# Last normalisation of five token tiles: product and offset split between ScalarE, VectorE and an adding DMA

## The reference, cut to what matters

```
x = layer_norm(ALPHA * x + mixer(x), ln1_g, ln1_b)
x = layer_norm(ALPHA * x + moe(x), ln2_g, ln2_b)

layer_norm(x, g, b) = (x - mean(x)) * rsqrt(var(x) + eps) * g + b
```

## Time and profile before

| | |
|---|---|
| median of three runs | 1285.62 us |
| profiled execution, its own time | 1287.54 us |
| its span, first to last instruction | 1285.7 us |
| TensorE busy | 1217.3 us, 95% |
| VectorE busy | 732.6 us, 57% |
| ScalarE busy | 579.2 us, 45% |
| GpSimd busy | 197.2 us, 15% |
| mean granted TensorE clock | 0.974 of full |
| the SP queue's transfers | 47.1% of the 16 DMA engines' span |
| GpSimd's transfers | 10.2% |

### The profile page before, as it was taken

One profiled execution on the slowest core, in us unless ns is written; L12 is line 12 of the kernel. 1 busy time (PEld: TensorE's weight loads), 2 busy tenths in 40 slices (PEclk: granted clock), 3 DMA queues, 4 the chain that ended last, 5 costly groups with the idle time before them and its releaser, 6 DMA issues.

```text
span 1285.7 us, 22049 instructions
## 1 busy us (share of the span) xinstructions
PE 1217.3 (95%) x8045; PEld 1090.7 (85%) x8045; DVE 732.6 (57%) x1790; ACT 579.2 (45%) x1416; POOL 197.2 (15%) x244
## 2 busy tenths in 40 slices
PE   6999999999999999998898999998799999999992
PEld 6998798888888888886677888897799999999892
DVE  3111455655665556556666887447566656656377
ACT  3221344544454444445543443220366766667464
POOL 0000001200210021011101122000213333333222
PEclk9999999999999999999798999899799999999996
DMA  5444664374536344565264333442799999999773
GB/s 185 160 127 129 168 144 100 82 185 94 130 88 174 95 108 104 138 146 169 70 199 165 132 142 115 159 153 66 248 304 277 282 288 280 270 280 292 195 291 131
DMA packets 157986, 220.69 MB, mean 172 GB/s; under 512 B 40608, under 2 KB 110496, under 8 KB 157856
## 3 DMA queue, kind: packets, MB, share of 16 engines
q1 hardware_dynamic: 147168, 180.80, 47.1%
q0 software_dynamic: 8192, 29.36, 10.2%
q10 hardware_dynamic: 2544, 9.44, 1.9%
HBM read 139.05 MB, written 50.63 MB: 148 GB/s over the span
## 4 chain that ended last, share of the span: by engine, by line
PE 82%; DVE 6%; issue 3%; ACT 3%; DMA 3%; DVEq 1%; SPq 1%; POOL 1%; ACTq 0%; POOLq 0%
PE bank L843 19%; PE bank L845 18%; PE bank L844 18%; PE bank L944 9%; PE bank L837 5%; PE bank L931 5%; PE bank L922 4%; PE bank L923 3%; PE bank L1064 2%; ACT b_work L1317 1%; DMA acc_scratch<-d_work,dstc 1%; DVE w_o L1677 1%; ACT w_o L1332 1%; DVE d_work L2086 1%; DVE d_work L2084 1%
## 5 line engine op out<-in xcount | busy, mean ns | idle before, releaser
L1317 ACT ACTIVATE b_work<-b_work 128x256 f32<-128x256 f32 (+3 forms) x288 | 148.0, 514 | 246.3 <-DVE b_work L1658 246.2
L843 PE MATMUL bank<-xgT_hi,w_gu_hi 128*128 128x224 f32 (+1 forms) x704 | 197.8, 281 | 4.4 <-ACT d_work L1550 2.3
L844 PE MATMUL bank<-xgT_lo,w_gu_hi 128*128 128x224 f32 (+1 forms) x704 | 196.5, 279 | 0.0
L845 PE MATMUL bank<-xgT_hi,w_gu_lo 128*128 128x224 f32 (+1 forms) x704 | 196.4, 279 | 0.0
L1667 DVE COPY b_work<-bank 128x256 f32<-128x256 f32 (+2 forms) x256 | 112.7, 440 | 116.8 <-PE bank L931 116.2
L843 PEld LDWEIGHTS bank<-xgT_hi,w_gu_hi 128*128 128x128 f32 x704 | 136.9, 195 | 6.6 <-issue 3.1
L2177 POOL CAST Q<-Q 128x512 fp32r<-128x512 f32 x48 | 52.2, 1118 | 576.0 <-DVE w_k_lo L1624 342.5
L844 PEld LDWEIGHTS bank<-xgT_lo,w_gu_hi 128*128 128x128 f32 x704 | 136.9, 194 | 0.7
L845 PEld LDWEIGHTS bank<-xgT_hi,w_gu_lo 128*128 128x128 f32 x704 | 136.9, 194 | 0.0
L931 PE MATMUL bank<-keep,b_work 128*128 128x128 f32 x608 | 115.8, 276 | 13.1 <-ACT b_work L1317 13.1
L931 PEld LDWEIGHTS bank<-keep,b_work 128*128 128x128 f32 x608 | 79.7, 140 | 51.0 <-ACT b_work L1317 22.5
(11 more groups left out here) (210 smaller groups left out, 2833.5 us busy)
## 6 DMA issues: line engine op xcount, KB each, us to landing
d_work<-in_w_gate SPq DMA_DIRECT2D x32, 512.0 KB, 8.7
d_work<-in_w_up SPq DMA_DIRECT2D x32, 512.0 KB, 9.6
d_work<-in_w_down SPq DMA_DIRECT2D x16, 1024.0 KB, 9.7
Q<-stage_hi SPq DMA_DIRECT2D x96, 128.0 KB, 2.4
Q<-stage_lo SPq DMA_DIRECT2D x96, 128.0 KB, 2.4
o_scratch<-b_work SPq DMA_DIRECT2D x36, 264.0 KB, 3.2
c_work<-o_scratch SPq DMA_DIRECT2D x12, 792.0 KB, 5.1
raw_w<-in_w_in SPq DMA_DIRECT2D x26, 256.0 KB, 4.2
```

What stands on the lines that cost most here:

```text
L843: nc.tensor.matmul(o, w_hi, x_hi, start=first, stop=False)
L844: nc.tensor.matmul(o, w_hi, x_lo, start=False, stop=False)
L845: return nc.tensor.matmul(o, w_lo, x_hi, start=False, stop=last)
L1317: nc.scalar.activation(prob[:, u % 2, 0:n], prob[:, u % 2, 0:n], ACT.Exp, scale=-1.0, bias=o[:, HD:HD + 1], accum_out=o[:, HD + 1:HD + 2])\
```

## The change

It has four parts. (1) Five tiles, 7, 5, 8, 9 and 10 (`Z_SUM`), are finished in another way: ScalarE's new `z_norm` makes (x - mean) * rstd2 in one pass over the tile, behind a tiny instruction for -mean * rstd2; VectorE's `z_out` makes only the product with g (one `tensor_tensor` where there were two instructions); and the offset b is added by the output itself. (2) For that, SP writes b into the output rows of the five tiles early, with five DMAs of 512 KB from the row `ln2_b` in DRAM, repeated 128 times, which stand in SP's list directly ahead of the zeros (L625). GpSimd later adds each finished tile to these rows with a DMA that accumulates (`add_out`): tile 7 behind the norm factor of tile 10, the other four behind that of tile 11. (3) The sum of tiles 6 to 11 is no longer a pass of ScalarE: `add_shared` puts out the sum of each half of the row, and two tiny ScalarE instructions with accumulators make the means. (4) The orders change: on VectorE `z_out(7)` stands between `add_shared` of tile 10 and that of tile 11; on ScalarE each `z_norm` stands behind the `z_stats` of the next tile.

```diff
+        Z_SUM = (7, 5, 8, 9, 10)
+        zparts = tri[:, 104:116].rearrange("p (t c) -> p t c", c=2)
+        shift = tri[:, 116:128]
@@ SP, ahead of the zeros and of pair(0)
+            for t in Z_SUM:
+                sp.dma_start(out_t[t], ln2_b.partition_broadcast(P)).then_inc(S["offsets_st"], 16)
+
             sp.wait_ge(S["zeros_ready"], 1)
@@ SP, end
             for n, t in enumerate(Z_ORDER):
-                sp.wait_ge(S["fin_ready"], n + 1)
-                sp.dma_start(out_t[t], base[:, t, :]).then_inc(S["out_st0"], 16)
-            sp.wait_ge(S["out_st0"], 16 * TILES)
+                if t not in Z_SUM:
+                    sp.wait_ge(S["fin_ready"], n + 1)
+                    sp.dma_start(out_t[t], base[:, t, :]).then_inc(S["out_st0"], 16)
+            sp.wait_ge(S["offsets_st"], 16 * len(Z_SUM))
+            sp.wait_ge(S["out_st0"], 16 * (TILES - len(Z_SUM)))
+            sp.wait_ge(S["sums_st"], 16 * len(Z_SUM))
@@ ScalarE, z_stats
-                nc.scalar.activation(zjunk, base[:, t, :], ACT.Copy, accum_out=zsum[:, c])
-                act.drain()
-                nc.scalar.activation(minus_mean[:, c], zsum[:, c], ACT.Copy, scale=-1.0 / D)
-                nc.scalar.activation(mean_32[:, c], zsum[:, c], ACT.Copy, scale=-1.0 / D / 32)
+                if t < 2 * EARLY:
...
+                else:
+                    nc.scalar.activation(zjunk[:, 0:2], zparts[:, t - 2 * EARLY, :], ACT.Copy, scale=-1.0 / D,
+                                         accum_out=minus_mean[:, c])
+                    nc.scalar.activation(zjunk[:, 2:4], zparts[:, t - 2 * EARLY, :], ACT.Copy, scale=-1.0 / D / 32,
+                                         accum_out=mean_32[:, c])
                 act.drain()
+            def z_norm(t):
+
+                c = slice(t, t + 1)
+                act.wait_ge(S["z_rstd"], Z_ORDER.index(t) + 1)
+                nc.scalar.activation(shift[:, c], minus_mean[:, c], ACT.Copy, scale=rstd2[:, c])
+                act.drain()
+                nc.scalar.activation(base[:, t, :], base[:, t, :], ACT.Identity, scale=rstd2[:, c], bias=shift[:, c])\
+                  .then_inc(S["z_norm"], 1)
@@ ScalarE, end
-            for t in (5, 8, 9, 10, 11):
-                z_stats(t)
+            z_stats(5)
+            z_norm(7)
+            z_stats(8)
+            z_norm(5)
+            z_stats(9)
+            z_norm(8)
+            z_stats(10)
+            z_norm(9)
+            z_stats(11)
+            z_norm(10)
@@ VectorE
-                    last = V.scalar_tensor_tensor(b, bank[4 + 2 * half + c][:], 1.0 / ALPHA, b, ALU.mult, ALU.add)
+                    sums = {"accum_out": zparts[:, 2 * (tile - EARLY) + half, c:c + 1]} if tile >= EARLY else {}
+                    last = V.scalar_tensor_tensor(b, bank[4 + 2 * half + c][:], 1.0 / ALPHA, b, ALU.mult, ALU.add, **sums)
@@ VectorE, z_out
+                if t in Z_SUM:
+                    dve.wait_ge(S["z_norm"], Z_SUM.index(t) + 1)
+                    V.tensor_tensor(base[:, t, :], base[:, t, :], ln2g, ALU.mult).then_inc(S["fin_ready"], 1)
+                    return
@@ VectorE, end
-            for half in range(2):
-                add_shared(end, EARLY + LATE - 1, half)
-            for t in (7, 5, 8, 9, 10, 11):
+            add_shared(end, EARLY + LATE - 1, 0)
+            z_out(7)
+            add_shared(end, EARLY + LATE - 1, 1)
+            for t in (5, 8, 9, 10, 11):
                 z_out(t)
@@ GpSimd
+            def add_out(t):
+
+                if t == Z_SUM[0]:
+                    pool.wait_ge(S["offsets_st"], 16 * len(Z_SUM))
+                pool.wait_ge(S["fin_ready"], Z_ORDER.index(t) + 1)
+                pool.dma_start(out_rows[t], base[:, t, :], accum_op=ALU.add).then_inc(S["sums_st"], 16)
+
@@ GpSimd, in the loop over Z_ORDER, behind the norm factor, and behind the loop
+                if t == Z_SUM[-1]:
+                    add_out(Z_SUM[0])
+            for t in Z_SUM[1:]:
+                add_out(t)
```

More of the change, by code:

```diff
@@ L360, in encoder_layer @@
             cum_need cum_made cum_read ej_ready id_need idm_made table_ready ids_col dst_col gathers_begun stores_begun g_ld late_ld
-            gcol_ready ln2_loaded z_var z_bn z_eps z_rstd fin_ready out_st0""".split()
+            gcol_ready ln2_loaded z_var z_bn z_norm offsets_st sums_st z_eps z_rstd fin_ready out_st0""".split()
         names += [f"acc_ld{t}" for t in range(TILES)]
@@ L1570, in z_stats @@
                 act.drain()
-                nc.scalar.activation(zjunk, base[:, t, :], ACT.Copy, accum_out=zsum[:, c])
-                act.drain()
-                nc.scalar.activation(minus_mean[:, c], zsum[:, c], ACT.Copy, scale=-1.0 / D)
-                nc.scalar.activation(mean_32[:, c], zsum[:, c], ACT.Copy, scale=-1.0 / D / 32)
+                if t < 2 * EARLY:
+                    nc.scalar.activation(zjunk, base[:, t, :], ACT.Copy, accum_out=zsum[:, c])
+                    act.drain()
+                    nc.scalar.activation(minus_mean[:, c], zsum[:, c], ACT.Copy, scale=-1.0 / D)
+                    nc.scalar.activation(mean_32[:, c], zsum[:, c], ACT.Copy, scale=-1.0 / D / 32)
+                else:
[3 more added lines that the diff above has]
+                                         accum_out=mean_32[:, c])
                 act.drain()
@@ L2256, in _ @@
             add_to_tokens(end)
+            out_rows = out.rearrange("(t p) d -> t p d", p=P)
+            def add_out(t):
[3 more added lines that the diff above has]
+                pool.dma_start(out_rows[t], base[:, t, :], accum_op=ALU.add).then_inc(S["sums_st"], 16)
             for n, t in enumerate(Z_ORDER):
```

## The result

The changed kernel is slower: 1302.86 us, median of five runs (1300.66 to 1305.16), against 1283.66 for the kernel before in five runs (1281.78 to 1286.1). The ratio is 1.0146 [1.0131, 1.0161], so 19 us. The prediction said 1292.1 and 1282 to 1298: the direction was right, the size lay outside the range.

What follows compares the result with a forecast made beforehand. VectorE was taken to bound the last stage, with the chain through TensorE before it. Beginning loses 10.4 us, end gains 3.9: +6.5 on the median 1285.62 gives 1292.1 us, range 1282 to 1298 for 8 in 10.

Steps and rivals of the forecast that it cites:

- The bound at the end: Last norms: VectorE bounds this stage; five fewer instructions remove 6.8 us, its chain ends at 1274.9, that branch gains 7.7.
- The sums: Ahead of the last shared product: shorter `z_stats` on ScalarE let the last Silu start earlier, of which 1.35 us arrive.
- The stall at the beginning: Attention start, 150 us: offsets ahead of `dup` into `KB` delay its landing and idle TensorE; 10.4 us lost (6.4 to 13.8).
- the clock term: After the stall near 160 us, TensorE restarts at 1.2 in place of 2.4 GHz: about 2.0 us lost (0 to 4).
- I take the slower middle, 8.4 us: Offsets in SP's queue near 150 us: 2.62 MB at 311 GB/s delay what follows by 8.4 us (6.4 to 9.8).
- The adding DMAs: End, GpSimd branch: four adding DMAs behind the last norm factor at 1271.5 end at 1281.8; gain 3.9 us (-1 to 7).
- I take 1.6 and 5.0, between the loaded rows and the plain store since the queues are empty here: End: each adding DMA costs GpSimd 1.6 us to issue and takes 5.0 us to landing.
- The "0.5" behind the landing: End: the span was to end 0.5 us behind the last adding DMA's landing, the last part of the sum 1281.8.
- The third rival: End: adding DMAs replace VectorE as bound, at 1.91 us each and 11.1 to landing; span end 1288.8, time 1299.1; chance 0.10.
- Behind it I see no stall that would take the delay up again: After the attention's beginning: the chain stays on TensorE for hundreds of us, so the beginning's delay is not regained.

Runs made afterwards that it cites:

- 14.0 alone: Kernel before plus only the five offset DMAs from the repeated `ln2_b` row, ahead of the zeros: 1300.72 us, ratio 1.0128.
- With distinct rows: Kernel before plus five DMAs ahead of the zeros, each copying 128 different rows of x instead of one repeated row: 1295.47 us, ratio 1.0088.
- three early additions with spread offsets: Changed kernel with offsets spread over attention passes, only tiles 7, 5, 8 finished the new way, adding DMAs issued earlier: 1277.52 us, ratio 0.9943.
- two early: Changed kernel with offsets spread over attention passes, only tiles 7 and 5 finished the new way, adding DMAs issued earlier: 1280.02 us, ratio 0.9968.
- Without the addition: Changed kernel with offsets spread over attention passes, GpSimd's five final DMAs writing tiles without adding: 1279.48 us, ratio 0.9965.

## Why the prediction was right or wrong

**The bound at the end: right.** VectorE's chain was the bound, and it shortened as said: its end was put at 1274.9 and came at 1274.1 in the time of the kernel before. So did ScalarE: the last `z_norm` was to end at 1270.7 and ended at 1282.74 - 12.62 = 1270.1. The cost of a `z_stats` and `z_norm` together was put at 3.5 us and measured 3.37 (1281.50 less 1278.13).

**The sums: right.** 1.35 us were to arrive of a shorter ScalarE list, and the wait fell by 1.35 us, 1.94 to 0.59. That TensorE's end came 3.0 us earlier owes 1.6 us to a lower clock that only the profile of the kernel before has.

**The stall at the beginning: mechanism right, rate wrong.** Queue, waiting engines and idle TensorE came as described, and the clock term was 1.8 us where 2.0 was said. The step that failed is "I take the slower middle, 8.4 us". It gave the offsets the rate of the stretch, 311 GB/s, with 9.8 as the upper bound from a copy between distinct rows. They took 12.5 us here and 14.0 alone, which is 2.62 MB at 210 and 187 GB/s. The nearest row for a repeated row had 374 GB/s, but that was a load into SBUF. With distinct rows the forecast held to 0.2 us. So the beginning lost 14.3 where 10.4 was said and 13.8 was the worst: 3.9 us.

**The adding DMAs: the price was put in the wrong place.** The prediction costed GpSimd's issue at 1.6 us each and gave every one 5.0 us to landing. The term was 1271.5 + 3 x 1.6 + 5.0 + 0.5 = 1281.8. In the time of the kernel before (less 12.62) the last issue began at 1271.7, 4.6 us earlier than the 1276.3 of the sum. From there to landing it took 13.3 us, 8.3 more than said, and behind the landing came 3.1 us and not 0.5, 2.6 more. In all 8.3 + 2.6 - 4.6 = 6.3 us, which turns a gain of 3.9 into a loss of 2.4. The step that failed is "I take 1.6 and 5.0, between the loaded rows and the plain store since the queues are empty here": the landing was taken as a latency that each DMA has for itself. It is throughput: each adding DMA of 512 KB holds all 16 DMA engines for about 3.0 us, so those issued 0.88 us apart queue behind each other. The "0.5" behind the landing failed too: it is what a store of SP's leaves, and behind a DMA of GpSimd's its `DRAIN` makes it 3.1. The third rival, at 0.10, named what happened, and put the end of the span at 1288.8 where it came at 1288.1 in the time of the kernel before. The closeness is luck: its last issue began 5.5 us too late, and its landing (11.1) and closing wait (0.5) were 2.2 and 2.6 too short; its reason, GpSimd's slow issues, is not what the runs show. "The queues are empty here" was true of what stood in them before, not of what the change puts there.

**The range.** Both errors have the same sign: 3.9 at the beginning and 6.3 at the end, less the 1.7 that came back. 6.5 + 3.9 + 6.3 - 1.7 = 15.0. The range took in the one or the other, not both. The rest of the 10.8 us between 1292.1 and 1302.86 is no mechanism: the profiled execution of the kernel before was 1.9 us above the median that the forecast was added to, and that of the changed kernel 0.3 below its own.

**Regained.** "Behind it I see no stall that would take the delay up again" was right as far as the profiles can tell: the 1.7 us that came back are within what they differ by in this stretch.

## What to carry to other kernels

Cost a DMA twice, as a latency and as time of the 16 DMA engines, and check the second against everything that is in flight in the last stretch: work given to an adding DMA is moved to a resource of less than half its usual speed (3.0 us of all engines in place of 1.3), and pays only as long as its last transfer lands some 2.5 us ahead of the last plain store. A transfer that nobody waits for still delays what stands behind it in its queue, so put it where the next `dup` is far, and in small portions. When a change has several parts, run them alone: here the sums gained 2.0 us, three early additions with spread offsets brought the gain to 6.9, and the whole as written lost 19. And compare a stage with several profiles that have it unchanged: that of the kernel before was 1.6 us longer in the last stage than four others.

## What the runs showed of the hardware

- DRAM to DRAM DMAs whose packets all read one 4 KB row (of `ln2_b`) are slower than the same packets from 16 rows (of x): 12.5 and 14.0 us of delay against 8.7 for 2.62 MB. In the same kernel before, a load of a repeated row into SBUF ran at 374 GB/s.
- A direct adding DMA from SBUF to DRAM, 512 KB: 0.88 us of GpSimd's time, 3.0 us of all 16 DMA engines, 5.5/8.6/13.3 us to landing where four follow each other, some 200 GB/s with all DMA engines busy. Plain ones from GpSimd: 0.53 to 0.65 us, 1.3 us of the engines, 3.0/3.8/5.0. SP's one plain store beside the adding ones (tile 11) took 8.8 us in place of 2.6 (view of line 836).
- GpSimd's closing `DRAIN` ends 2.7 to 2.9 us behind the landing of its last DMA, adding or plain, in all seven kernels in which it issues some at the end. Where that comes last, the execution ends 3.0 to 3.1 us behind this landing (six kernels); behind SP's last store it is 0.4 to 0.5 us (the kernel before, and two early). Without the addition, the view of line 116 has:

```profile
L116 POOLq DRAIN  x1: 7846/7846/7846, 1269.7 to 1269.7; - x1
```

This ends at 1277.5, and the last landing was at 1269.7 + 5.0 = 1274.7.
